# A hybrid DeltaNet layer: 32x32 transposes on VectorE in the blockwise inverse, and its matrix masked ahead, once per level, by GpSimd

## What is computed

```python
a = -jnp.where(strict, jnp.einsum('bhncd,bhnkd->bhnck', kb, k) * decay, 0.0)

def fwd_sub(i, tm):
    row = tm[..., i, :]
    return tm.at[..., i, :].set(row + jnp.einsum('...j,...jk->...k', row, tm))

tinv = lax.fori_loop(1, CHUNK, fwd_sub, a) + jnp.eye(CHUNK, dtype=F32)
...
def step(state, xs_i):
    u_i, w_i, qk_i, qd_i, kd_i, cd_i = xs_i
    v_new = u_i - jnp.einsum('bhcd,bhde->bhce', w_i, state)
    o = (jnp.einsum('bhcd,bhde->bhce', qd_i, state)
         + jnp.einsum('bhck,bhke->bhce', qk_i, v_new))
    state = state * cd_i[..., None, None] + jnp.einsum('bhcd,bhce->bhde', kd_i, v_new)
    return state, o
```

## Time and profile before

| | before |
|---|---|
| median of three runs | 2594.44 us (2594.44 to 2596.92) |
| the profiled execution, and its span | 2589.97 us, 2588.3 us |
| `delta_stage` in the profile | about 1245 to 1920 us |
| PE busy, PE weight loads busy | 2282.7 us, 1909.6 us |
| DVE, ACT, POOL busy | 1107.8, 717.0, 397.0 us |

### The profile page before, as it was taken

How to read it: one execution, slowest core, us unless ns; L and a number is a source line. 1 busy time by engine, 2 the same in 40 slices (tenths; PEclk the granted TensorE clock), 3 DMA queues, 4 the chain that set the end, 5 groups by cost and what they waited for, 6 DMA issues and landing times. The chain is left out here.

```text
span 2588.3 us, 31160 instructions
## 1 busy us (share of the span) xinstructions
PE 2282.7 (88%) x12032; PEld 1909.6 (74%) x12032; DVE 1107.8 (43%) x1682; ACT 717.0 (28%) x1160; POOL 397.0 (15%) x251
## 2 busy tenths in 40 slices
PE   6999999999999999994399998999956765599998
PEld 6788888888888888883288887888943433488887
DVE  7844444443441122212355554555427665322222
ACT  5411111111111011100345554444234344311111
POOL 3200000000000000000455554554000000000000
PEclk9999999999999999997699999999968897799999
DMA  7322222222222222211301221220050121544442
GB/s 234 133 98 73 73 73 73 73 73 73 73 72 73 73 73 73 73 49 36 119 26 63 74 74 58 74 74 17 9 166 25 53 66 63 200 150 143 144 143 86
DMA packets 74063, 220.02 MB, mean 85 GB/s; under 512 B 7488, under 2 KB 25024, under 8 KB 69744
## 3 DMA queue, kind: packets, MB, share of 16 engines
q1 hardware_dynamic: 63136, 179.35, 20.8%
q0 software_dynamic: 10832, 39.39, 4.0%
HBM read 174.02 MB, written 44.70 MB: 85 GB/s over the span
## 5 line engine op out<-in xcount | busy, mean ns | idle before, releaser
L73 PE MATMUL pr_acc<-x_hi,pr_w_lo 128*128 128x512 f32 (+1 forms) x1760 | 675.8, 384 | 25.9 <-DVE pr_w_lo L386 23.3
L75 PE MATMUL pr_acc<-x_hi,pr_w_hi 128*128 128x512 f32 (+1 forms) x1760 | 674.3, 383 | 0.0
L74 PE MATMUL pr_acc<-x_lo,pr_w_hi 128*128 128x512 f32 (+1 forms) x1760 | 674.2, 383 | 0.0
L73 PEld LDWEIGHTS pr_acc<-x_hi,pr_w_lo 128*128 128x128 f32 x1760 | 334.2, 190 | 91.6 <-issue 18.3
L74 PEld LDWEIGHTS pr_acc<-x_lo,pr_w_hi 128*128 128x128 f32 x1760 | 334.3, 190 | 63.8 <-issue 0.2
L75 PEld LDWEIGHTS pr_acc<-x_hi,pr_w_hi 128*128 128x128 f32 x1760 | 334.1, 190 | 63.6
L314 ACT ACTIVATE pr_w_hi<-pr_w_raw 128x1024 fp32r<-128x1024 f32 x118 | 124.8, 1059 | 758.4 <-PE pr_acc L75 739.3
L464 DVE TENSOR_TENSOR pr_padded<-pr_acc,pr_rstd 128x512 f32<-128x512 f32 x80 | 55.2, 692 | 501.5 <-PE pr_acc L75 501.3
L73 PE MATMUL ou_acc<-ou_w_hi,ou_m_lo 128*128 128x512 f32 x512 | 200.0, 391 | 46.8 <-ACT ou_w_hi L1678 46.8
L74 PE MATMUL ou_acc<-ou_w_lo,ou_m_hi 128*128 128x512 f32 x512 | 199.8, 390 | 0.0
L75 PE MATMUL ou_acc<-ou_w_hi,ou_m_hi 128*128 128x512 f32 x512 | 199.7, 390 | 0.0
(11 more groups left out here) (217 smaller groups left out, 2917.5 us busy)
## 6 DMA issues: line engine op xcount, KB each, us to landing
pr_w_raw<-in_w_in SPq DMA_DIRECT2D x118, 512.0 KB, 4.9
ou_w_raw<-in_w_out SPq DMA_DIRECT2D x32, 1024.0 KB, 4.8
proj_scratch<-pr_res POOLq DMA_DIRECT2D x51, 512.0 KB, 5.0
dl_qk<-proj_scratch SPq DMA_DIRECT2D x8, 1024.0 KB, 4.9
dl_grow<-gate_rows SPq DMA_DIRECT2D x8, 1024.0 KB, 7.3
dl_brow<-gate_rows SPq DMA_DIRECT2D x8, 1024.0 KB, 10.2
ou_w_raw<-mixed_scratch SPq DMA_DIRECT2D x16, 512.0 KB, 4.7
ou_x_in<-in_x SPq DMA_DIRECT2D x8, 1024.0 KB, 7.4
```

Source lines behind the costliest of these rows:

```text
L73: pe.matmul(out, w_lo, x_hi, start=first, stop=False)
L74: pe.matmul(out, w_hi, x_lo, start=False, stop=False)
L75: return pe.matmul(out, w_hi, x_hi, start=False, stop=last)
```

## The change

Levels 0 to 4 (blocks of up to 32) lose T and take_t. VectorE transposes D itself, in blocks of 32x32 (`turn`), reading the alternating blocks straight from `dt` and writing `d`; a block of D never leaves its 32x32 tile of the diagonal up to s = 32. Level 5 keeps T on PE and take_t on ACT. The mask moves from the product to the matrix: behind the sum M, GpSimd writes M times the mask of each level, six instructions, into `first_levels` (levels 0 to 3) and over the two halves of `mt` (levels 4 and 5). take_z becomes a plain copy and moves from VectorE to ScalarE, to the places at which take_t stood; ScalarE has both at level 5. PE's wait for the scan of the head before moves from T to Z of level 0, and Z of each level waits for its masked matrix (`e_level`).

```diff
+        first_levels = n.sb("first_levels", [P, 4, NC, P])
+        mt_level = [first_levels[:, i] for i in range(4)] + [mt[:, NC:NT], mt[:, 0:NC]]
...
+        def rows_d(parity, chunk, count, level):
+            return alternating(dt[:, parity, chunk], NC * P, count * P, LEVELS[level])
...
+            def take_z(h, level):
+                for b in range(4):
+                    act.wait_ge(s_z, h * LZ + (4 * level + b + 1))
+                    act.activation(zz[:, 2 * b:2 * b + 2], ring[:, b, 0:2 * P].rearrange("p (a n) -> p a n", n=P),
+                                   ACT.Copy).then_inc(s_zd, 1)
...
-                take_t(h, 0)
+                take_z(h, 0)
...
-                take_t(h, 5)
+                take_t(h)
+                take_z(h, 5)
...
                 pool.tensor_tensor(mt[:, 0:NC], mt[:, 0:NC], mt[:, NC:NT], ALU.add).then_inc(e_both, 1)
+                pool.wait_ge(e_both, g + 1)
+                for level in range(L):
+                    pool.tensor_tensor(mt_level[level], mt[:, 0:NC],
+                                       masks[:, level, None, :].to_broadcast([P, NC, P]), ALU.mult).then_inc(e_level, 1)
...
-            def take_z(h, level, b):
-                dve.wait_ge(s_z, h * LZ + (4 * level + b + 1))
-                dve.tensor_tensor(zz[:, 2 * b:2 * b + 2], ring[:, b, 0:2 * P].rearrange("p (a n) -> p a n", n=P),
-                                  masks[:, level, None, :].to_broadcast([P, 2, P]), ALU.mult).then_inc(s_zd, 1)
+            def turn(h, parity, level, b):
+                if level == 0:
+                    dve.wait_ge(e_d1, h * 4 + 4)
+                else:
+                    dve.wait_ge(s_id, h * LZ + (4 * (level - 1) + b + 1))
+                dve.transpose(d[:, 2 * b:2 * b + 2].rearrange("p a n -> p (a n)"),
+                              rows_d(parity, 2 * b, 2, level)).then_inc(s_td, 1)
...
             def slot(h, parity, more, before):
                 g, q = h + 1, 1 - parity
+                for b in range(4):
+                    turn(h, parity, 0, b)
                 for level in range(L):
-                    for b in range(4):
-                        take_z(h, level, b)
...
                     for b in range(4):
                         take_i(h, parity, level, b)
+                        if b > 0 and level + 1 < L - 1:
+                            turn(h, parity, level + 1, b - 1)
+                    if level + 1 < L - 1:
+                        turn(h, parity, level + 1, 3)
...
             def products_z(h, level, b):
-                pe.wait_ge(s_td, h * LT + (4 * level + b + 1))
-                if level == 0 and b == 0:
-                    pe.wait_ge(e_both, h + 1)
+                if level == L - 1:
+                    pe.wait_ge(s_tl, h * 4 + (b + 1))
+                else:
+                    pe.wait_ge(s_td, h * LT + (4 * level + b + 1))
+                if level == 0 and b == 0 and after_first(h):
+                    pe.wait_ge(s_vd, h * NC)
+                    pe.wait_ge(s_sd, h * KS)
+                if b == 0:
+                    pe.wait_ge(e_level, h * L + (level + 1))
                 for i in range(2):
-                    last = pe.matmul(ring[:, b, bass.ts(i, P)], mt[:, 2 * b + i], d[:, 2 * b + i], start=True, stop=True)
+                    last = pe.matmul(ring[:, b, bass.ts(i, P)], mt_level[level][:, 2 * b + i], d[:, 2 * b + i],
+                                     start=True, stop=True)
...
-                for b in range(4):
-                    transposes(h, parity, 0, b)
                 for level in range(L):
...
-                    if level < L - 1:
+                    if level == L - 2:
                         for b in range(4):
-                            transposes(h, parity, level + 1, b)
+                            transposes(h, parity, b)
```

More of the change, by code:

```diff
@@ L623, in delta_stage @@
         L = len(LEVELS)
[L624 removed]
+        LT, LZ = 4 * (L - 1), 4 * L
         KS = 2 * (NC - 1)
@@ L783, in slot @@
                     end_squares(h - 1)
-                take_t(h, 0)
+                take_z(h, 0)
                 if more:
                     roots(g, 1)
-                take_t(h, 1)
+                take_z(h, 1)
                 if more:
@@ L791, in slot @@
                     end_roots(h - 1)
-                take_t(h, 2)
+                take_z(h, 2)
                 if more:
@@ L796, in slot @@
                     row_exps(g)
-                take_t(h, 3)
+                take_z(h, 3)
                 if more:
@@ L800, in slot @@
                     decays(g, 0, 5)
-                take_t(h, 4)
+                take_z(h, 4)
                 if more:
                     decays(g, 5, 5)
-                take_t(h, 5)
+                take_t(h)
+                take_z(h, 5)
                 if more:
@@ L1065, in end_sums, with transposes @@
                               start=True, stop=True).then_inc(f_nm, 1)
[L1067 to L1074 removed]
+            def transposes(h, parity, b):
+                pe.wait_ge(s_id, h * LZ + (4 * (L - 2) + b + 1))
                 for i in range(4):
```

21 lines of the change are left out of this document (6 added, 15 removed).

## The result

The changed kernel takes 2604.32 us (median of 20 runs, 2595.72 to 2616.27), the kernel before in the same sessions 2595.07 (20 runs, 2589.39 to 2599.53): a ratio of 1.0040, 95% interval 1.0029 to 1.0052. It is slower by 0.4%, where 0.3% faster was forecast. The profiled execution took 2602.19 us against 2589.97.

The account below looks back on a forecast made before the run. PE was taken as the bound where nothing interrupts, ACT and DVE waits at levels 0 to 3; -10.2 for middle slots, -3.5 for slot 7, +6 for the clock sum to -7.7, about 2587 us, range 2580 to 2592.

Parts of the forecast that it names:

- the term for TensorE's clock: Middle slots: longer PE waits bring one more fall of the clock per slot at 1.0 us, +6 in all.
- slot 0: First slot: the mask delays Z by 2.4 us, later gains are of the same size, so 0 in sum.
- The start, +0.7: Start of a slot: Z of level 0 waits for its mask and starts 0.7 us later.
- Price of a transpose, 0.42 us: VectorE's transposes: about 0.42 us each, 0.33 from start to start, so VectorE's total work stays unchanged.
- Rival B: VectorE's transposes cost twice as much, 0.66 us from start to start; 2594 to 2600 us, chance 0.13.
- A free level, 4.1 us: Levels where nothing interrupts take 4.1 us instead of 5.34, -1.2 us each.
- Levels 0 to 2, -0.9: Slots 1 to 6, up to I of level 2: at best -1.9 us, `to_rows` gives some back, middle taken, -0.9.
- rival D: `columns` under the masks: its small VectorE operations wait for GpSimd on the shared port; 2625 us or more, chance 0.07.
- Level 3, -0.9: Level 3: the earlier gain of 0.9 us stays, as `beta_column` still waits for POOL's 5.67 us pair.
- Rival E: Level 3: `beta_column` runs before POOL's second L845, 1.9 us sooner in six slots; 2575 us, chance 0.10.
- Level 3 to 4, -0.8: From take_i of level 3 to I of level 4: 5.0 us instead of 5.85, -0.8.
- Rival C: Starts of levels 0, 1 and 4: the clock falls at most long waits; 2601 to 2611 us, chance 0.24.

Follow-up runs that it names:

- e2: The changed kernel with five of the six small operations of `columns` moved from VectorE to ScalarE; ratio 1.0047 to the kernel before.
- e9: e6 with the six masks added on GpSimd and read by nobody; ratio 1.0060 to the kernel before.
- e10: e9 with five of the six operations of `columns` moved to ScalarE; ratio 0.9888 to the kernel before.
- e3: The changed kernel with `beta_column` ahead of the normalization and the gate's product behind level 3's take_i and turns; ratio 0.9945 to the kernel before.
- e5: The changed kernel with unread transposes added on TensorE in the waits at the slot's start and ahead of level 4's Z; ratio 1.0019 to the kernel before.
- e6: The changed kernel with transposes on VectorE kept, but VectorE masking the product as before and no masks on GpSimd; ratio 0.9807 to the kernel before.
- c1: The changed kernel with the edits of e1, e2 and e3 together; ratio 0.9850 to the kernel before.
- e1: The changed kernel with GpSimd adding the identity to D's first half right behind that half's mask; ratio 1.0073 to the kernel before.

## Why the prediction was wrong

The prediction gave 0.32 to a slower kernel. **The step that failed** is the term for TensorE's clock, +6 us for one more fall per middle slot at 1.0. The trace shows 14 slow stretches in the six slots where the kernel before had 3, 1.8 more per slot, and an estimate puts them at 14 us. Next to it, levels 0 to 3 gained 0.7 us a slot instead of 1.7, and slot 0 lost 5.2 instead of nothing.

Slot 3's start is counted from 0.55 us behind the start of the scan's last group: 1513.51 before (where T stood), 1525.49 after.

The estimate: in slot 3, I of level 4 starts 40.05 us behind the slot's start (1565.54 less 1525.49), where it was 39.21 (1552.72 less 1513.51), +0.84 instead of -1.7. Z of level 4 at half speed is 1.56 of that; the rest is -0.7. Six slots at -0.7 make -4.3, and they measured +9.7, which leaves 14 for the clock. Between -7.7 and the +12.3 of the spans lie 20.0 us: about 8 by the clock, 6 by levels 0 to 3, 5.2 by slot 0, 0.6 from ahead of slot 0 and 0.3 by slot 7.

*The start, +0.7:* right. Z starts 2.6 us behind it instead of 1.8, behind a wait of 2.39.

*Price of a transpose, 0.42 us:* right, 418 ns. Rival B is out. The estimate of 444 ns from the Trainium skill ("VectorE: DVE Perf Modes", The three transpose paths) was close, 6% above the trace.

*A free level, 4.1 us:* right. I of slot 7 starts at 1842.65, 1846.88 and 1851.12, 4.2 apart. Slot 7 gave 3.2 of the forecast 3.5.

*Levels 0 to 2, -0.9, and rival D:* failed too. The text let two instructions of `columns` wait and called that "nothing lost"; four do, 8.9 us, and take_i of level 0 starts at 1534.92, 2.6 us later than I (from 1531.65) allowed it at 0.65 behind. D's mechanism was seen, and its chance of 0.07 was too low for it. In this kernel it cost PE little: Z of level 1 waits 0.6 to 0.7 us in slots 3 and 6, and in slots 1, 2 and 5, where Z of level 0 ran slow, not at all. The rule used ("an operation waits when it meets POOL") was known from the earlier trace rows; what was missed is that the masks keep POOL busy without a gap under the whole of `columns`, while before POOL's two L829 end early. e2 shows that freeing `columns` alone is no cure; e9 and e10 show its price where ScalarE's list is free of copies (PE waits 5.3 us or more for it in five of e9's six slots). I of level 2 is 24.1 us behind the slot's start, against 24.3 before: -0.2 instead of -0.9.

*Level 3, -0.9:* failed too. The wait was forecast at 3.9 and is 4.25, but take_i of level 3 comes 33.5 us behind the slot's start, where it had been 33.4 (1546.87 less 1513.51): +0.2. Rival E did not happen. e3, which forces its order and also moves the gate's product out of the way, gains 25 us where E promised 11.

*Level 3 to 4, -0.8:* the pace was right, the clock was not: from take_i to I of level 4 it is 6.5 us instead of 5.0, Z at half speed making 1.6 of it.

*The clock, +6:* too small. The prediction counted one more fall a slot at 1.0; there were 1.8 more, and Z of level 4 lost 1.5 to 1.7 us in each slot. Slot 5 took 1.8 us more than slot 3 for the same instructions. e5 bears the cause out, not the whole size: 5 us of the median for two of three places. The sum of the middle slots was to be -4.2 with the term and was +9.7. Slot 0 was put at 0 and lost 5.2: behind 17.2 us without work on PE, Z and the sums of norms ran in 3.75 and 3.14 us instead of 1.95 and 1.88 (before, T alone ran slow there, 3.37), and `to_rows` waited 4.16 us for `unit`.

The forecast treated the change as one. e6 and e9 show it as two of opposite sign, -1.9% and about +2.3%. The transposes were undervalued: without the masks and ScalarE's copies a middle slot gains 7.0 us on average. Nearly all of it comes by level 2, where ACT's roots start earlier; the forecast had booked only gains of a change with ACT's copy in front of the roots. Rival C was nearest, in time (2601 to 2611) and in mechanism: its places, the starts of levels 0 and 4 and the sums of level 1, are where the clock was low, and it counted two to three a slot, where the trace has 2.3. The waits themselves stand behind GpSimd and ScalarE, as e3, e9 and c1 show: taking the wait at level 3 away gives 25 us with what the clock gives back. Open is how the loss splits between `columns`, ACT's list, the masks' wait at the start and the clock behind each, since these close one path together.

The Trainium skill ("SBUF — State Buffer", Who interferes with whom) names the kinds of instruction that waited: copies and tensor_scalar in the two-port modes, and tensor_tensor with both inputs in SBUF. The runs agree in the main: of these, four of six took 1.9 to 2.3 us beside POOL in slot 3, two 0.16, while take_i, reading one input from PSUM, kept 0.38 us, and `turn`, one input, kept 0.42. It also says that issue order decides who blocks; in e1 all six waited, in the changed kernel four.
